# Expert gates scattered by indirect DMA instead of built by one-hot matmuls, in a fused attention and PEER layer

## The reference

```python
s1 = jnp.einsum('thd,hnd->thn', qry[:, :, 0], sub_keys1)      # 8 heads, 128 keys each
s2 = jnp.einsum('thd,hnd->thn', qry[:, :, 1], sub_keys2)
v1, i1 = lax.top_k(s1, 16);  v2, i2 = lax.top_k(s2, 16)
cand = v1[..., :, None] + v2[..., None, :]
cand_idx = i1[..., :, None] * 128 + i2[..., None, :]
top_s, pos = lax.top_k(cand.reshape(..., 256), 16)
idx, gate = take_along_axis(cand_idx, pos), softmax(top_s)
act = gelu(x . expert_down[idx]) * gate                       # 16 experts for each token and head
out = sum(act * expert_up[idx])
```

## Time and profile before

| | |
|---|---|
| median of 3 runs | 3580.58 us |
| the profiled execution's own time | 3585.94 us |
| its span, first to last instruction | 3584.1 us |
| TensorE busy | 3540.5 us, 99% |
| VectorE, ScalarE, GpSimd busy | 60%, 40%, 57% |
| mean granted TensorE clock | 0.997 |
| DMA, mean over the span | 243 GB/s; 325 to 377 GB/s from about 1600 us on |

### The profile page before, as it was taken

The page is one execution under the profiler, slowest core; times in us unless marked ns, Lnnn a source line. Parts: engine busy times, 40 slices in busy tenths (PEclk is TensorE's granted clock), DMA queues, the critical chain, the costliest instruction groups (busy, mean ns, idle before and its releaser), DMA issues.

```text
span 3584.1 us, 50859 instructions
## 1 busy us (share of the span) xinstructions
PE 3540.5 (99%) x20069; PEld 3218.9 (90%) x20069; DVE 2136.7 (60%) x3752; ACT 1418.0 (40%) x1782; POOL 2025.9 (57%) x696
## 2 busy tenths in 40 slices
PE   7999999999999999999999999999999999999999
PEld 5777777777788888899999999999999999999999
DVE  6333344444685139896666666533577777777774
ACT  5544545555422223333444444333333333333332
POOL 2333333333344434477666666677777777777774
PEclk9999999999999999999999999999999999999999
DMA  3322222222334332388989888899999899999994
GB/s 153 139 101 98 96 95 88 97 82 94 120 141 184 110 116 94 126 309 325 357 324 353 322 337 332 347 346 377 360 361 357 348 348 357 363 358 354 354 353 156
DMA packets 181721, 871.95 MB, mean 243 GB/s; under 512 B 15520, under 2 KB 69024, under 8 KB 90400
## 3 DMA queue, kind: packets, MB, share of 16 engines
q1 hardware_dynamic: 59376, 399.48, 30.2%
q0 software_dynamic: 46224, 336.61, 23.7%
q10 hardware_dynamic: 75936, 133.28, 10.1%
HBM read 805.32 MB, written 69.21 MB: 244 GB/s over the span
## 4 chain that ended last, share of the span: by engine, by line
PE 62%; issue 22%; DVE 6%; POOL 5%; DMA 3%; ACT 1%; DVEq 0%; POOLq 0%; SPq 0%; ACTq 0%
PE ps L1514 59%; POOL w_lo L348 5%; DVE ps L1304 4%; PE ps L1744 2%; DMA expert_rows<-down_rows,idx 1%; DMA w_e_raw<-w_stream 1%; DVE h_dense L1434 1%; POOL w_e_lo L355 1%; DVE expert_rows L1291 0%; PE ps L1678 0%; DMA g_dram<-gate_buf 0%; DVE hn_lo L1134 0%; POOL expert_rows L383 0%; ACT w_e_hi L721 0%; DMA x_raw<-x_t 0%
## 5 line engine op out<-in xcount | busy, mean ns | idle before, releaser
L355 POOL TENSOR_TENSOR w_e_lo<-w_e_raw,w_e_hi 128x2048 fp32r<-128x2048 f32 x256 | 1183.5, 4624 | 521.9 <-ACT w_e_hi L721 520.3
L348 POOL TENSOR_TENSOR w_lo<-w_raw,w_hi 128x2048 fp32r<-128x2048 f32 x115 | 538.5, 4682 | 931.9 <-ACT w_hi L415 931.9
L1514 PE MATMUL ps<-sn_hi,w_e_hi 128*128 128x352 f32 x2048 | 669.5, 327 | 7.9 <-POOL w_e_lo L355 5.2
L1514 PE MATMUL ps<-act_hi,w_e_hi 128*128 128x352 f32 x2048 | 664.7, 325 | 5.3 <-DVE h_dense L1434 3.2
L1514 PE MATMUL ps<-act_lo,w_e_hi 128*128 128x352 f32 x2048 | 661.5, 323 | 0.0
L1514 PE MATMUL ps<-act_hi,w_e_lo 128*128 128x352 f32 x2048 | 661.4, 323 | 0.0
L1514 PE MATMUL ps<-sn_hi,w_e_lo 128*128 128x352 f32 x2048 | 661.0, 323 | 0.0
L1514 PE MATMUL ps<-sn_lo,w_e_hi 128*128 128x352 f32 x2048 | 658.7, 322 | 0.0
L721 ACT ACTIVATE w_e_hi<-w_e_raw 128x2048 fp32r<-128x2048 f32 x256 | 489.3, 1911 | 197.6 <-DMA w_e_raw<-w_stream 123.4
L1291 DVE SCALAR_TENSOR_TENSOR expert_rows<-expert_rows,ps 128x2048 f32<-128x2048 f32 x160 | 363.3, 2284 | 202.6 <-DMA expert_rows<-down_rows,idx 112.2
L1514 PE MATMUL ps<-xn_hi,w_hi 128*128 128x512 f32 x1088 | 447.2, 411 | 18.1 <-DVE xn_lo L922 18.0
(11 more groups left out here) (257 smaller groups left out, 4850.5 us busy)
## 6 DMA issues: line engine op xcount, KB each, us to landing
w_e_raw<-w_stream SPq DMA_DIRECT2D x256, 1024.0 KB, 8.1
w_raw<-w_stream SPq DMA_DIRECT2D x116, 1024.0 KB, 4.8
gel_dram<-gel_all ACTq DMA_DIRECT2D x32, 704.0 KB, 9.5
g_dram<-gate_buf ACTq DMA_DIRECT2D x11, 2048.0 KB, 13.2
gel_in<-gel_dram ACTq DMA_DIRECT2D x32, 704.0 KB, 6.3
g_exp<-g_dram ACTq DMA_DIRECT2D x32, 704.0 KB, 14.5
gate_dram<-g_raw ACTq DMA_DIRECT2D x32, 256.0 KB, 2.0
g_in<-gate_dram ACTq DMA_DIRECT2D x16, 512.0 KB, 6.1
```

The costliest lines, as they stand in the source:

```text
L348: nc.gpsimd.tensor_tensor(wlo[s][:, :], raw[s][:, :], whi[s][:, :].bitcast(F32), ALU.subtract).then_inc(lo_ready, 1)
L355: nc.gpsimd.tensor_tensor(e_lo[j % 4][:, :], e_raw[j % 4][:, :], e_hi[j % 3][:, :].bitcast(F32), ALU.subtract).then_inc(lo_ready, 1)
L1514: m = mm(ps[:, bank, 0:width], lhs[:, w], r, start=(n % (3 * per) == 0), stop=(n % (3 * per) == 3 * per - 1))
```

## The change

The gate matrix is no longer computed. An array of the same size in HBM, [key 2, key 1, token] flat, is set to zero during the attention stage by 11 stores of 2 MB from the bias tile, which is blank until then (ScalarE's queue, two in each of five loop turns and one behind them). VectorE works out the flat position of each gate of the 352 tokens, and GpSimd scatters the gates: one indirect DMA for each head, block of 128 tokens (the third block has 96) and rank k, so 8 x 3 x 16 = 384 of them, each writing 128 or 96 single elements and adding them to what is there. Those of one head and block go without waits; before the 16 of the next head, GpSimd waits for those of the same block of the head before. One scatter is due in each of tiles 20 and 21, and six in each tile from 22 to 85. For the 66 tiles from 22 to 87 VectorE, not GpSimd, makes the low half, as the first thing of its tile t - 2. GpSimd takes the low halves up again with tile 88. The transposes, one-hots, gate matmuls, gate copies and gate stores are gone, and the loads of the gates are contiguous, 5632 bytes a partition instead of 11 pieces of 512.

```diff
+UNITS = [(h, b) for h in range(HEADS) for b in range(SPARSE)]
+SCATTERS = [(h, b, k) for h, b in UNITS for k in range(TOPK)]
+SLOW, FAST = 1, 6
+ZEROINGS = 11
+T_LOW = T_GATES + 2
+SCATTER_TILE = [T_GATES + n // SLOW if n < SLOW * (T_LOW - T_GATES) else T_LOW + (n - SLOW * (T_LOW - T_GATES)) // FAST
+                for n in range(len(SCATTERS))]
+T_LOW_END = SCATTER_TILE[-1] + 3
...
-        g_dram = nc.dram_tensor("g_dram", [GATE_GROUPS, P, KEYS * GT], F32).ap()
+        g_dram = nc.dram_tensor("g_dram", [KEYS * KEYS * TD, 1], F32).ap()
+        g_rows = g_dram.rearrange("(p n) o -> p (n o)", p=P)
...
+            def scatter(h, b, k):
+
+                if (h, b, k) == (0, 0, 0):
+                    pool.wait_ge(zeroed, 16 * ZEROINGS)
+                if k == 0:
+                    pool.wait_ge(scat_ready, 1)
+                    if h > 0:
+                        pool.wait_ge(scattered[b], 16 * TOPK * h)
+                rows_, c = min(P, TD - P * b), PAIRS * b + TOPK * h + k
+                gate = tv_all[0:rows_, c:c + 1]
+                nc.gpsimd.indirect_dma_start(g_dram, bass.IndirectOffsetOnAxis(scat_idx[0:rows_, c:c + 1], 0), gate,
+                                             None, compute_op=ALU.add).then_inc(scattered[b], 16)
...
-                if t + 1 < 2 * EXPERT_TILES:
+                if t + 1 < 2 * EXPERT_TILES and not T_LOW <= t + 1 < T_LOW_END:
+                    if t + 1 == T_LOW_END:
+                        pool.wait_ge(lo_ready, B_DOWN + T_LOW_END)
                     low(t + 1)
...
+                for unit, tile in zip(SCATTERS, SCATTER_TILE):
+                    if tile == t:
+                        scatter(*unit)
...
+            def zero_gates(part):
+
+                blank_row = bias.rearrange("p h c -> p (h c)").rearrange("p (o c) -> p o c", o=1).to_broadcast([P, 4, 1024])
+                act.dma_start(g_rows[:, bass.ds(4096 * part, 4096)].rearrange("p (o c) -> p o c", o=4),
+                              blank_row).then_inc(zeroed, 16)
...
                 if isinstance(n, int):
                     spread_bias(2 * (n - 1) + 1)
+                else:
+                    zero_gates(2 * i)
+                    zero_gates(2 * i + 1)
...
-            def store_gates(g):
...
-            def gates_out(n):
...
                 act.dma_start(gel_in[s][:, :], gel_dram[g]).then_inc(up_in[s], 16)
-                act.dma_start(g_exp[s][:, :].rearrange("p (g c) -> p g c", g=GATE_GROUPS),
-                              g_view[:, :, bass.ds(g, 1), :].rearrange("p g k c -> p (g k) c")).then_inc(up_in[s], 16)
+                act.dma_start(g_exp[s][:, :], g_rows[:, 4 * TD * g:4 * TD * (g + 1)]).then_inc(up_in[s], 16)
...
             vec.memset(negm[:, :], 0.0).then_inc(warm, 1)
+            vec.memset(bias, 0.0).then_inc(blank, 1)
...
+            vec.scalar_tensor_tensor(out=by_block(scat_f), in0=by_block(i1_all), scalar=float(TD), in1=token,
+                                     op0=ALU.mult, op1=ALU.add)
+            v.drain()
+            vec.scalar_tensor_tensor(out=scat_f[:, :], in0=i2_all[:, both], scalar=float(KEYS * TD), in1=scat_f[:, :],
+                                     op0=ALU.mult, op1=ALU.add)
+            v.drain()
+            vec.tensor_copy(scat_idx[:, :], scat_f[:, :]).then_inc(scat_ready, 1)
...
-            def one_hots(n):
...
+            def low_of_tile(j):
+
+                b = B_DOWN + j
+                v.wait_ge(hi_ready, b + 1)
+                if j == T_LOW:
+                    v.wait_ge(lo_ready, b)
+                vec.tensor_tensor(e_lo[j % 4][:, :], e_raw[j % 4][:, :], e_hi[j % 3][:, :].bitcast(F32),
+                                  ALU.subtract).then_inc(lo_ready, 1)
...
             for t in range(T_GATES, EXPERT_TILES):
-                for n in range(N_GATES):
-                    if GATE_TILE[n] == t:
-                        one_hots(n)
...
+                if T_LOW <= t + 2 < T_LOW_END:
+                    low_of_tile(t + 2)
...
-            def turn_values_and_i1():
...
-            def turn_i2():
...
-            def gates(n):
```

More of the change, by code:

```diff
@@ L51 @@
 T_EXP = 14
-T_TURN = 17
+T_COPY = 19
 T_GATES = 20
-GATE_TILE = [T_GATES + 5 * n // 6 for n in range(N_GATES)]
 EARLY_PAIRS = 6 * TOPK
@@ L830, in _ @@
                 peer_hi(t + 2)
-                for n in range(N_GATES):
-                    if GATE_TILE[n] == t:
-                        gates_out(n)
                 down(t)
                 if t == T_FIRST:
-                    act.wait_ge(g_dma, 16 * GATE_GROUPS)
-                    act.wait_ge(idx_ready, 2)
+                    for b in range(SPARSE):
+                        act.wait_ge(scattered[b], 16 * PAIRS)
                     act.wait_ge(gate_x_in, 16 * COPIES)
@@ L1364, in _ @@
             vec.tensor_tensor(per_head(tv_all), per_head(tv_all), one_each(sum_ps), ALU.mult).then_inc(tk_done, 1)
-            for j in range(17, 20):
+            both = slice(0, PAIRS * SPARSE)
+            by_block = lambda t: t[:, both].rearrange("p (b c) -> p b c", b=SPARSE)
+            token = cols[:, C_TOK:C_TOK + SPARSE].rearrange("p (b o) -> p b o", o=1).to_broadcast([P, SPARSE, PAIRS])
+            vec.scalar_tensor_tensor(out=by_block(scat_f), in0=by_block(i1_all), scalar=float(TD), in1=token,
+                                     op0=ALU.mult, op1=ALU.add)
@@ L1366, in _ @@
+            v.drain()
[3 more added lines that the diff above has]
+            vec.tensor_copy(scat_idx[:, :], scat_f[:, :]).then_inc(scat_ready, 1)
+            vec.tensor_copy(gate_3[:, :], tv_all[:, sparse])
+            for j in range(17, FIRST_ROWS):
                 dot(j)
             v.drain()
-            vec.tensor_copy(gate_3[:, :], tv_all[:, sparse])
@@ L1720, in _ @@
             scaled = operand(sn_hi, sn_lo, w=TD)
[L1722 to L1725, removed]
-            def turn_values_and_i1():
-                pe.wait_ge(tk_done, 1)
-                turn_topk(tv_all, GB)
-                turn_topk(i1_all, GB + 1)
-            def turn_i2():
-                pe.wait_ge(gthi_ready, 1)
-                turn_topk(i2_all, GB)
-            def gates(n):
[L1740 to L1746, removed]
-            for t in range(EXPERT_TILES):
[L1749 to L1756, removed]
+            for t in range(EXPERT_TILES):
+                extras = {6: [lambda: key_scores(CT - 1, 1)]} if t == 0 else None
                 stream(B_DOWN + t, t % 2, [(MAIN + t % 2, (down_out, t - 1), scaled)], extras,
                        before=(lambda c: (slo_ready, c + 1)) if t == 0 else None, width=TD)
-            pe.wait_ge(g_sb, N_GATES)
             def turn_sum():
@@ L1863, in lay_out @@
     small[:, C_EPS] = EPS
+    small[:, C_TOK:C_TOK + SPARSE] = np.arange(P)[:, None] + P * np.arange(SPARSE)[None, :]
     keys_t = np.stack([a["peer_sub_keys1"][0], a["peer_sub_keys2"][0]], 1).transpose(3, 0, 1, 2).reshape(P, 16 * KEYS)
```

68 lines of the change are left out of this document (10 added, 58 removed).

## The result

| | before | after |
|---|---|---|
| median of 4 runs each | 3580.64 us | 3912.86 us (3905.55 to 3915.98) |
| ratio, 95% interval | | 1.092 (1.090 to 1.094) |
| the profiled execution | 3585.94 us | 3915.98 us |
| mean granted TensorE clock | 0.997 | 0.955 |

What follows compares the result with a forecast made beforehand. TensorE bounds the kernel before; afterwards GpSimd's scatters decide. Tile 88's start -8, tiles 88 to 92 -5.3, transposes -0.9, zeroing +2, loads -1, clock +2: -11 us, 3575 profiled, forecast 3570 us, range 3498 to 3680.

Steps and rivals of the forecast that it cites:

- (g): GpSimd's queue before tile 88: 384 scatters, 1.24 us each (1.12 with 96 rows), the term that decides.
- (f): VectorE forms low halves of tiles 22 to 87, 2.29 us each; fits, but GpSimd can stop TensorE through VectorE.
- rival 2: Low halves on VectorE and GpSimd's scatters hold each other up: +152 us, 3722 us; chance 0.08.
- rival 1: GpSimd's queue, low halves 21 to 88: a scatter costs more than a gather, up to +157 us, 3727; chance 0.27.
- (a): TensorE loses gate matmuls, 1.10 us in each of 72 tiles, plus tile 20's extra and transposes: 83 us together.
- (b): VectorE loses its one-hot instructions, 3.0 us for each of 88 steps; worth nothing, since it waited for TensorE.
- (c): ScalarE loses 99 gate copies, most 1.14 us, and 11 stores; hidden, so worth nothing.
- (d): Gate loads of the last stages become contiguous instead of landing after 14.5 us; TensorE hardly waits there: -1 us.
- (e): Eleven 2 MB zeroing stores on ScalarE's queue in the attention stage delay weight loads: +2 us, bounds 0 and 25.
- The restart at tile 88: At tile 88 TensorE meets GpSimd's lag at once, and its granted clock is low after the wait: +2 us.
- Rival 3: DMA engines pay an HBM read and write per scattered element: at 100 ns, +190 us, 3760 us; chance 0.08.
- rival 4: Scatters under 1.02 us let GpSimd keep pace; TensorE stays the bound, all 83 us won: 3498 us; chance 0.17.

Runs made afterwards that it cites:

- that run: Half the scatters (ranks 0 to 7) and VectorE's low-half instruction reading its second operand from PSUM, against the kernel after: 3513.18 us, 0.981 of before.

## Why the prediction was wrong

**The step that failed is (g), the price of a scatter.** It took "the gather's 1.24 us, the nearest row", and put the high end at "1.24 + 0.37 = 1.61 us". The runs show 1.27 us (0.97 + 0.30) for a scatter that stores: for that the nearest row was right. Adding costs 0.59 us more, and its 1.86 us (1.56 + 0.30) lie beyond the high end. The bound's reasoning was "if that is paid twice", the index's 0.37 us; nothing in the trace tied the cost of adding to the cost of an index, so it was no bound. It was 235 of the 343 us.

**The second is the cover of (f).** "A tile then asks VectorE for 2.29 us and 4/3 row products ... it fits" was right for VectorE and overlooked GpSimd: the low half runs in its own 2.29 us each time, and what it stops is the queue that bounds the stage. That was rival 2, with 0.08. Its price was too high (95 us in the durations, 91 and 92 between the runs, not 152), since an instruction of GpSimd that is already 0.22 us under way isn't stopped, and those that start late in a low half lose only its rest. Its condition, whether a DMA instruction counts as a reader, is settled for GpSimd's indexed ones: they do. That it is the read of the index, and nothing else in the instruction, is argued and not shown; that instructions already under way are left alone fits a read at their start. The rule that the prediction cited from the Trainium skill's page "SBUF — State Buffer" (section "Who interferes with whom") thus holds for these instructions too. The same section explains why a `tensor_tensor` left DMA unhindered in a probe of its own by the notion, marked there as inferred, that descriptor generation needs the write side alone; with an index read from SBUF the runs here say otherwise, and the measurement decides.

**A term that was put at nothing.** VectorE's computation of the flat positions stands neither in (f) nor anywhere else in the sum. In the kernel after it took 5 us (1643.8 to 1648.9), about 3.4 of them because GpSimd held up its first instruction, and it delayed gathers, low half 19 and with it TensorE by a wait of 3.1 us. It is the smallest of the three errors, at most 4.5 of the 8 us of GpSimd's late start. The start was also read from the trace with the transposes in it, so that their 0.9 us could not come off tile 88 as well.

**Both rivals came true together.** The prediction priced each alone, 3727 at the dear end of rival 1 and 3722 for rival 2, and its range ended at 3680. Their sum was never formed, although they act on the same queue and so add without any cover: 3727 + 152 = 3879 was in its own numbers.

**Point by point.** (a) TensorE's gain: 83 us forecast; with GpSimd out of the way the profiled execution is 75.7 us shorter. The 1.10 us a tile came: tile 21 ended at 1683.10 before and at 1685.37 in that run, tile 92 at 2306.76 and at 2230.64, so 71 tiles gained 78.4 us, 1.10 each. What was missing is ahead of them: tile 21 ends 2.3 us later than before, where the forecast had it end at 1679.0, 4.1 us earlier. Of these 6.4 us, tile 18 brings 1.8 (1657.71 against 1655.88), with a stage ahead of it that starts 1.2 us later in this execution. The other 4.6 are lost between the ends of tiles 18 and 21: TensorE waits 2.8 us at tile 19 for a low half that the computation of the flat positions delayed, and its granted clock is 0.83 from 1660 to 1670. (b) and (c) hold: nothing waits for VectorE's and ScalarE's removed work. (d) The gates land after 9.0 us instead of 14.5, but the 1 us put on it doesn't show: from the end of tile 92 to the end of the span it took 1277.4 us before and 1277.7 in that run. (e) The zeroing was put at +2 us; no cost shows. GpSimd's last low half of the attention and projection stages starts at 1467.33 instead of 1466.20, but its 21st already started 1.1 us later (276.85 against 275.74). The transfers of the weights land as before:

```profile
w_raw<-w_stream SPq DMA_DIRECT2D x116, 1024.0 KB, 4.8
...
g_dram<-bias ACTq DMA_DIRECT2D x11, 2048.0 KB, 12.3
...
g_exp<-g_dram ACTq DMA_DIRECT2D x32, 704.0 KB, 9.0
```

(f) 2.29 us per low half holds. That GpSimd stops TensorE through VectorE, and that low half 88 is where its lag is met, holds in every run with 384 scatters: ScalarE's Gelu copy of tile 88 comes after 23 to 42 us of idle time in each. The restart at tile 88, put at +2 us, shows in these stretches:

```profile
2560.00:2590.00 30.00, 0.00 (x0) 0.00 (x0) 9.19 (x8) 2.36 (x2) 24.49 (x20) 0.59 0.64 169
2590.00:2600.00 10.00, 5.96 (x22) 5.96 (x23) 2.54 (x3) 0.00 (x0) 9.52 (x4) 0.53 0.70 247
2600.00:2610.00 10.00, 10.00 (x65) 10.00 (x64) 6.64 (x6) 2.27 (x2) 9.64 (x5) 1.00 0.88 313
```

After 34 us without a matmul the granted clock is 0.53, near the lower of its two levels (1.2 of 2.4 GHz), and 22 matmuls take 5.96 us, 0.27 each. From 2600 on it is full. Tile 88 took 10.4 us (2594.0 to 2604.4) instead of 7.68: 2.8 us. DMA: the forecast took 11 ns an element and kept 46; the estimate above is 35, and the packets took 31 to 42. This term had no effect on the time that shows, but was nearer its upper end. The forecast's 11 ns came from packets that don't add; in the run with plain stores the scatters' packets, 32 for each scatter, took 9 to 14 ns. Rival 3 at 100 ns and rival 4, a scatter under 1.02 us, are out.

## What to carry to other kernels

Before work is moved onto an engine that issues DMAs, count its instructions against the time of a tile: here 6 scatters x 1.86 + 1.33 gathers x 1.28 = 12.9 us went into a tile of 7.68 us, while 1 or 2 scatters a tile fitted and won 30 us. Count the small preparations too: 5 us of index arithmetic on VectorE made TensorE wait 3 us. An operation that the trace doesn't show in its own form (a DMA that adds) has no upper bound from a relative that doesn't do the new part; give it room, or time one first. Rivals that load the same queue add up, so form their sum before the range is closed, and let an engine that helps a bound engine read one of its operands from PSUM if it can.

## What the runs showed that was not expected

- An indexed DMA instruction of 128 single elements holds GpSimd 0.97 us when it stores and 1.56 us when it adds, 0.30 us apart. With 96 rows the adding one takes 1.42: 4.4 ns a row between these two sizes, so by this estimate about 1.0 us of it doesn't depend on the rows. Fewer rows in an instruction would hardly help.
- It is stopped while VectorE runs an instruction with two SBUF operands, if it starts during it, and VectorE is not stopped by it (its low halves take 2.28 to 2.36 us): the mean of 95 us over 66 low halves is 1.4 us each. Beside the same instruction with one operand in PSUM no scatter is longer than 1.62 us.
- An element that is added costs the DMA engines about 35 ns. Six adding scatters a tile at 7.68 us would take 6 x 117 x 35 ns = 25 of 16 x 7.68 = 123 engine-us, 0.20 of share on top of 0.89: a quicker GpSimd would have met the DMA engines next. That is worked out, not run.
- A scatter that adds leaves 144 packets on GpSimd's queue (128 rows) or 112 (96 rows), one that stores 32:

```profile
q0 software_dynamic: 97424, 336.82, 25.2%
...
q0 software_dynamic: 58512, 336.82, 23.4%
```

  The first line is of the kernel after, the second of the run with plain stores; the difference, 38912, is 256 x 112 + 128 x 80. The number of packets alone doesn't make the 0.59 us, since a gather leaves 144 as well and takes 0.94 to 1.00 us.
- Left open: what in an adding instruction takes the 0.59 us, and whether scatters of the first head of a block, which could store since nothing is there yet, would give back 32 x 0.59 + 16 x 0.51 = 27 us in the kernel after; it wasn't tried.
